# Two-block transformer kernel: the weight split, the exponentials and the scaling of each attention unit cut into halves

## The reference

```python
# first block: 16 query heads, 2 key heads, blocks of 128 queries, window 128, one sink per head
scores = einsum(q, k_window) * 0.125 ; masked to 0 <= i - j < 128
probs  = softmax(concat([scores, sink]))[..., :-1]
out    = einsum(probs, v_window)
# second block: 8 heads, chunks of 64 queries, 576 keys at most, a learned relative bias
scores = einsum(q, k_band) * 0.125 + bias
probs  = softmax(scores) ; out = einsum(probs, v_band)
```

## Time and profile before

| What | Value |
| --- | --- |
| Time of the kernel before, median of 3 runs | 815.47 us (815.34 to 817.68) |
| The profiled execution | 815.34 us, its span 813.6 us |
| TensorE busy | 796.6 us, 98% of the span |
| VectorE busy | 592.4 us, 73% |
| ScalarE busy | 498.6 us, 61% |
| Mean granted TensorE clock | 0.998 of full speed |
| First attention, units 0 to 5 | about 42 to 138 us of the span |
| Second attention, units 6 to 8 | about 571 to 603 us |

### The profile page before, as it was taken

The page is one execution under the profiler, slowest core; times in us unless marked ns, Lnnn a source line. Parts: engine busy times, 40 slices in busy tenths (PEclk is TensorE's granted clock), DMA queues, the critical chain, the costliest instruction groups (busy, mean ns, idle before and its releaser), DMA issues. The chain is left out here.

```text
span 813.6 us, 14276 instructions
## 1 busy us (share of the span) xinstructions
PE 796.6 (98%) x5952; PEld 744.8 (92%) x5952; DVE 592.4 (73%) x772; ACT 498.6 (61%) x752; POOL 15.8 (2%) x36
## 2 busy tenths in 40 slices
PE   8999999999999999999999999999999999999996
PEld 8988879999999889999998889999788999999885
DVE  5575686648766877887878897897768877787463
ACT  6777788568837475344344266856657776666452
POOL 3000000000200000000000000000000000000000
PEclk9999999999999999999999999999999999999999
DMA  8873634446453577889798993635352865646611
GB/s 301 285 252 111 207 104 156 155 155 226 162 183 105 160 254 232 264 292 298 253 300 279 354 358 110 234 133 155 104 173 68 256 205 168 197 137 200 233 52 52
DMA packets 105680, 161.15 MB, mean 198 GB/s; under 512 B 4480, under 2 KB 51856, under 8 KB 105616
## 3 DMA queue, kind: packets, MB, share of 16 engines
q1 hardware_dynamic: 105472, 159.97, 59.8%
q10 hardware_dynamic: 144, 0.26, 0.1%
HBM read 159.16 MB, written 1.06 MB: 197 GB/s over the span
## 5 line engine op out<-in xcount | busy, mean ns | idle before, releaser
L1073 DVE TENSOR_TENSOR wL<-raw,wH 128x2048 fp32r<-128x2048 f32 (+2 forms) x134 | 283.0, 2118 | 122.7 <-ACT wH L695 119.2
L1672 PE MATMUL ps<-p1H,wH 128*128 128x256 f32 x1256 | 359.2, 286 | 1.7 <-DVE p1L L1073 0.8
L1672 PE MATMUL ps<-p1L,wH 128*128 128x256 f32 x1256 | 355.3, 283 | 0.0
L1672 PE MATMUL ps<-p1H,wL 128*128 128x256 f32 x1256 | 355.3, 283 | 0.0
L695 ACT ACTIVATE wH<-raw 128x2048 fp32r<-128x2048 f32 (+1 forms) x120 | 223.1, 1866 | 122.1 <-PE ps L1672 65.9
L1672 PEld LDWEIGHTS ps<-p1H,wH 128*128 128x128 f32 x1256 | 240.8, 192 | 4.8 <-issue 3.5
L1672 PEld LDWEIGHTS ps<-p1L,wH 128*128 128x128 f32 x1256 | 240.9, 192 | 0.3 <-issue 0.2
L1672 PEld LDWEIGHTS ps<-p1H,wL 128*128 128x128 f32 x1256 | 240.8, 192 | 0.0
L1675 PE MATMUL ps<-wH,zH 128*128 128x512 f32 x168 | 65.4, 389 | 0.0
L1675 PE MATMUL ps<-wH,zL 128*128 128x512 f32 x168 | 65.4, 389 | 0.0
L1675 PE MATMUL ps<-wL,zH 128*128 128x512 f32 x168 | 65.4, 389 | 0.0
(11 more groups left out here) (284 smaller groups left out, 974.5 us busy)
## 6 DMA issues: line engine op xcount, KB each, us to landing
raw<-in_w_in SPq DMA_DIRECT2D x37, 1024.0 KB, 5.1
raw<-in_w_ada SPq DMA_DIRECT2D x24, 1024.0 KB, 5.2
raw<-in_w_up SPq DMA_DIRECT2D x44, 512.0 KB, 4.8
raw<-in_w_ffn_gate SPq DMA_DIRECT2D x22, 512.0 KB, 4.5
raw<-in_w_ffn_up SPq DMA_DIRECT2D x22, 512.0 KB, 5.6
raw<-in_w_ffn_down SPq DMA_DIRECT2D x10, 1024.0 KB, 5.3
raw<-in_w_down SPq DMA_DIRECT2D x10, 1024.0 KB, 5.0
raw<-in_w_out SPq DMA_DIRECT2D x8, 1024.0 KB, 5.1
```

The lines of the kernel that those rows point to most:

```text
L1073: return v.tensor_tensor(o, a, b, op)
L1672: last = mm(ps[:, t[1], 0:T], wt[:, slot, k, t[2]:t[2] + P], at_[:, k0 + k, :], start=st, stop=en)
```

## The change

Five edits, all around the attention units; no product, transfer or buffer is added or taken away.

1. In units 0 to 5 the split's ScalarE copy is cut into two of 128 x 1024 (`half_hi`). The first stands where the whole one stood, the second stands behind the exponentials, under a new event ("rest", name, part, u) at the end of `X`. In units 6 to 8 ScalarE still copies the whole panel ahead of the exponentials.
2. In all units but unit 6 the difference on VectorE is cut likewise (`half_lo`): the first half between the maxima and the scaling, the second behind the scaling. `w_lo` is counted up by the second half alone. In unit 6 the difference stays whole.
3. `probs` is raised twice for each unit, after each half of its exponentials, and the sink's exponential (all heads at once) stands between the halves. All waits on `probs` are renumbered.
4. The scaling is done twice, each time for half the heads: `SU + ES` (first attention), reciprocal, and a multiplication of 128 x 512, each raising `pn`.
5. TensorE waits for `pn` before turn 0 and again before turn 4, where it waited once before turn 0; its wait for the yT and pt semaphores now stands ahead.

The diff, cut to its core:

```diff
-HALVED = {("q0", 0): 7, ("out1", 1): 8}
+HALVED = {("q0", 0): 7, ("out1", 1): 14}
...
-                + [("split", name, part), ("scale", u)])
+                + [("split", name, part, u), ("scale", u), ("rest", name, part, u)])
...
+            def half_hi(q, x):
+
+                i = SIDX["w", q]
+                if x == 0:
+                    act.wait_ge(on.raw[i % NRAW], landed[i])
+                    act.wait_ge(*USED[q - NHL])
+                nc.scalar.activation(wH[:, q % NHL, 2 * x:2 * x + 2, :], raw[:, i % NRAW, 2 * x:2 * x + 2, :],
+                                     ACT.Copy).then_inc(on.w_hi if x else on.first_hi, 1)
+
...
                 elif k == "split":
-                    split_hi(PIDX[e[1:]] + AHEAD)
+                    if e[3] < NU1:
+                        half_hi(PIDX[e[1:3]] + AHEAD, 0)
+                    else:
+                        split_hi(PIDX[e[1:3]] + AHEAD)
+                elif k == "rest":
+                    if e[3] < NU1:
+                        half_hi(PIDX[e[1:3]] + AHEAD, 1)
...
-                    ins.then_inc(on.probs, 1)
-                    if kind == 1:
-                        act.wait_ge(on.dsink, u + 1)
-                        nc.scalar.activation(ES[:, u % 2, 0:nh], DS[:, u % 2, 0:nh], ACT.Exp).then_inc(on.esink, 1)
+                        if h % (nh // 2) == nh // 2 - 1:
+                            ins.then_inc(on.probs, 1)
+                        if h == nh // 2 - 1 and kind == 1:
+                            act.wait_ge(on.dsink, u + 1)
+                            nc.scalar.activation(ES[:, u % 2, 0:nh], DS[:, u % 2, 0:nh], ACT.Exp).then_inc(on.esink, 1)
...
+            def half_lo(q, x, u):
+
+                i = SIDX["w", q]
+                if x == 0 and u < NU1:
+                    dve.wait_ge(on.first_hi, KP + 3 + u + 1)
+                else:
+                    dve.wait_ge(on.w_hi, q - AHEAD + 1)
+                ins = tt(wL[:, q % NHL, 2 * x:2 * x + 2, :], raw[:, i % NRAW, 2 * x:2 * x + 2, :],
+                         wH[:, q % NHL, 2 * x:2 * x + 2, :].bitcast(F32), ALU.subtract)
+                if x:
+                    ins.then_inc(on.w_lo, 1)
+
...
                 elif k == "split":
-                    split_lo(PIDX[e[1:]] + AHEAD)
+                    if e[3] == NU1:
+                        split_lo(PIDX[e[1:3]] + AHEAD)
+                    else:
+                        half_lo(PIDX[e[1:3]] + AHEAD, 0, e[3])
+                elif k == "rest":
+                    if e[3] != NU1:
+                        half_lo(PIDX[e[1:3]] + AHEAD, 1, e[3])
...
-                    dve.wait_ge(on.probs, u + 1)
-                    if kind == 1:
-                        dve.wait_ge(on.esink, u + 1)
-                        step(tt(SU[:, u % 2, 0:nh], SU[:, u % 2, 0:nh], ES[:, u % 2, 0:nh], ALU.add))
-                    step(v.reciprocal(RD[:, u % 2, 0:nh], SU[:, u % 2, 0:nh]))
-                    p = PR[u].rearrange("p (h b) n -> p h (b n)", h=nh)
-                    tt(p, p, RD[:, u % 2, 0:nh].unsqueeze(2).broadcast_to([P, nh, nk * P]), ALU.mult).then_inc(on.pn, 1)
+                    for x in range(2):
+                        hs = slice(x * nh // 2, (x + 1) * nh // 2)
+                        dve.wait_ge(on.probs, 2 * u + x + 1)
+                        if kind == 1:
+                            dve.wait_ge(on.esink, u + 1)
+                            step(tt(SU[:, u % 2, hs], SU[:, u % 2, hs], ES[:, u % 2, hs], ALU.add))
+                        step(v.reciprocal(RD[:, u % 2, hs], SU[:, u % 2, hs]))
+                        p = PR[u].rearrange("p (h b) n -> p h (b n)", h=nh)[:, hs]
+                        tt(p, p, RD[:, u % 2, hs].unsqueeze(2).broadcast_to([P, nh // 2, nk * P]),
+                           ALU.mult).then_inc(on.pn, 1)
...
-                        pe.wait_ge(on.probs, u)
+                        pe.wait_ge(on.probs, 2 * u)
...
-                    pe.wait_ge(on.pn, u + 1)
...
                     for b in range(8):
+                        if b % 4 == 0:
+                            pe.wait_ge(on.pn, 2 * u + b // 4 + 1)
                         last = tr(pt67[:, b * P:(b + 1) * P], PR[u][:, b, :])
```

More of the change, by code:

```diff
@@ L1406, in _ @@
                     if u > 1:
-                        dve.wait_ge(on.probs, u - 1)
+                        dve.wait_ge(on.probs, 2 * u - 2)
                     s = sc45[:, 0:nh * nk * P]
@@ L1839, in _ @@
                         pe.wait_ge(on.yT_done, NU1)
-                        pe.wait_ge(on.probs, NU1)
+                        pe.wait_ge(on.probs, 2 * NU1)
                     else:
```

## The result

| | Time, median (range) | Ratio to before, 95% interval |
| --- | --- | --- |
| Before, beside it | 815.9 us (815.28 to 817.68, 6 runs) | |
| After | 810.55 us (809.3 to 812.18, 6 runs) | 0.993 [0.9914, 0.9945] |
| The profiled execution of after | 809.31 us, span 807.6 us, clock 0.997 | |

What follows compares the result with a forecast made beforehand. TensorE, busy 98% of the span, was taken to bound the kernel, so only its waits could be won: 815.34 us minus 5.4 for seven losses, plus 0 and 0, gives 809.9, said as 810.0 us; range 809.0 to 813.3.

Steps and rivals of the forecast that it cites:

- The ceiling: TensorE's turns waiting for VectorE's scaling, six units of the first attention and unit 6: at most 5.4 us to win.
- A loss of up to 0.54 + 0.42 = 0.96 us is gone by this alone: Scaling in halves: last pn 0.54 us earlier, needed only at the fifth turn, 0.42 later; only unit 1 (1.26) lies above.
- The fifth turn's 0.42 us: TensorE needs the last scaled half only for its fifth turn, four turns or 0.42 us after the first.
- The split in halves, 0.5 us in unit 1: ScalarE's halved weight copy ends before the negative maximum, so unit 1's exponentials start 0.5 us earlier.
- The second halves are hidden, 1.3 us to spare in unit 7: Second halves put behind cost nothing; tightest is unit 7, w_lo at 585.8, TensorE at its panel at 587.1.
- Rival 2: Second halves not hidden, panels of units 7 and 8 late: 812.4 us; chance 0.17 together with rival 1 in part.
- The added instructions are free: VectorE's added 0.75 us and ScalarE's 0.2 us a unit stay off the path while chains start with TensorE's scores.
- Rival 1: Added instructions fall on the path, 4.5 us back: 814.6 us; whole or another hiding mechanism 0.14, partly or rival 2 0.17.
- The price of a cut: VectorE's weight difference cut in two: 0.157 us more by the skill's rule, 0.15 by the rows.
- The second wait at 0: TensorE's second wait on pn inside the turns costs 0; upper bound 0.17 us, nine times, 1.5 us.
- Rival 3, late loads: SyncE's loads start later because w_lo comes 2 to 3 us later in six units: 825 us; it or another slower, 0.05.
- The sum: Whole kernel: 815.34 us minus 5.4, plus 0 and 0, gives 809.9; 810.0 us said.

Runs made afterwards that it cites:

- experiment 1: Changed kernel with the weight split whole and ahead again on ScalarE and VectorE, exponentials, scaling and turns still in halves: 814.03 us, ratio 0.9967.
- experiment 3: Changed kernel, but TensorE waits once, ahead of turn 0, for both halves of the scaling: 811.28 us, ratio 0.9945.
- experiment 2: Changed kernel with exponentials, scaling and turns whole again, the weight split still in halves: 814.79 us, ratio 0.9986.
- experiment 6: Changed kernel with the first half of VectorE's weight difference computed two more times in unit 7 alone: 812.33 us, ratio 0.9946.
- experiment 5: Changed kernel with the first half of VectorE's weight difference computed two more times in each of units 0 to 5: 812.82 us, ratio 0.9935.
- experiment 7: Changed kernel, but TensorE waits for pn ahead of each of the eight turns: 811.2 us, ratio 0.9931.
- experiment 8: Changed kernel, second attention's scores wait for each head pair's own k2 tile, not the last ("by pairs"): 810.57 us, ratio 0.9916; run again, 809.03 us.

## Why the prediction was right, and which step of it failed

- *The ceiling*, seven waits for the scaling, 5.4 us: right. All of it was won and nothing came back.
- *"A loss of up to 0.54 + 0.42 = 0.96 us is gone by this alone"*, said of the scaling in halves: wrong. Alone it left 3.45 us (experiment 1). The step took the last multiplication as 0.54 us shorter with the same 0.44 us before it. That holds where ScalarE's last exponential ends last (unit 0, where 0.12 was left of 0.76). Where VectorE itself is late, from its whole difference, the first half's 1.0 us stands in the way and the last half ends 0.4 us later than before. The prediction had seen that units 2, 3 and 5 waited for VectorE's difference, and passed over it because their losses "lie under 0.96 anyway"; of unit 4 it said that it had the pattern of unit 1, and by the rows shown above it had that of units 2, 3 and 5. The second edit covered the error: the halved split takes 1.07 us off VectorE there.
- *The fifth turn's 0.42 us*: it was in the sum for every unit; it is needed in three and worth 0.7 us (experiment 3).
- *The split in halves, 0.5 us in unit 1*: right for the place (the exponentials start 0.04 us after the negative maximum) and nearly for the size (0.41 in experiment 2). Its larger work was in units 2 to 5, where it wins 2.3 of 2.6 us by itself (experiment 2) and the scaling in halves none (experiment 1).
- *The second halves are hidden, 1.3 us to spare in unit 7*: right, 1.44 by the trace, 1.4 by experiment 6. Rival 2 is out.
- *The added instructions are free*: right. VectorE's 3.9 us more did not show, nor did 14.6 more in experiment 5, but for 0.34 in unit 5. Rival 1 is out.
- *The price of a cut*: the rows of the changed kernel, count, busy us and mean ns by form, give 2 x 1222 - 2293 = 151 ns for a difference cut in two. By the rule of the Trainium skill (*VectorE: DVE Perf Modes*, "The TRN2 errata") it is 157, and the trace agrees within 6 ns.

```profile
L1089 DVE TENSOR_TENSOR wL<-raw,wH 128x2048 fp32r<-128x2048 f32 x106 | 242.6, 2293 | 103.6 <-ACT wH L695 103.1
L1089 DVE TENSOR_TENSOR wL<-raw,wH 128x1024 fp32r<-128x1024 f32 x32 | 38.9, 1222 | 11.9 <-ACT wH L695 8.8 <-ACT wH L691 2.7
```

- *The second wait at 0*: right (experiment 7). Its upper bound, 0.17 us each, was the price of a wait that isn't fulfilled.
- *Rival 3, late loads*: no wait for a load of a weight shows in TensorE's waits after the change.
- *The sum*: 810.0 forecast, 810.55 and 810.41 measured. At 0.997 and above the kernel takes 809.3 to 809.4, lower than forecast by the shorter blocks of turns (0.3) and the input's 0.28; at 0.994 and 0.995 it takes 810.2 to 812.2. The forecast took one profiled execution's clock for all, and it is luck that two errors of opposite sign left it within 0.6 us. It is luck too that the wrong step above did no harm: the sum only needed both edits together to clear all seven units.

## What to carry to other kernels

Halving the last step of a chain helps only where the engine that does it has been waiting; where that engine is itself late, the first half's fixed part is added in front, and work of its own must move behind to pay for it. So find for each unit what ends the wait of the last step before summing over units with one number, and when two edits go together, work each out alone. Where the runs of one kernel spread by some microseconds, look at the granted clock stretch by stretch before comparing medians; its mean also counts stretches in which TensorE has nothing to do.

## What the runs showed of the hardware that was not expected

- The TensorE clock fell to 0.50 for up to some 7 us at the same place of the program in some executions and not in others, during or after two blocks of sixteen 32-column products in which TensorE is shown as busy (3.85 us of 4 in the execution of experiment 8, 486 to 490 us). From the turns of unit 0 to those of unit 6 the executions with it took longer by 1.07 us (experiment 6) and, the 0.7 us by pairs allowed for, by 2.6 (experiment 8). Of whole runs before the change the fastest take 814.9 to 815.4 us at 0.998 and 0.999, the slowest 818.4 to 819.8 at 0.993 to 0.995. With 128 columns in these products no run of six was under 0.997. Idle time at that place does not bring it on by itself: in experiment 7 TensorE was busy only 1.28 us of the 2 from 488 to 490 us, and the clock stayed at 1.00 behind it. Why it falls in one execution and not in the next stays open.
- A product of 32, 64 or 128 columns in f32 costs nearly the same at that place: 1.71, 1.74 (485.63 to 487.37 at 64) and 1.79 us for sixteen. Widening to 128 costs 0.08 us a block.
- Eight turns of 128 columns between products of 256 take 0.79 to 0.80 us when they start on time and 0.82 to 0.85 when they start late, so there a wait costs some 0.05 us more than its late start. Behind the scores of the second attention it does not: 0.85 us in unit 7 without a wait, 0.82 to 0.85 in unit 6 with one.
- A fulfilled semaphore wait on TensorE costs nothing that a block of eight shows: 0.79 to 0.80 us with one wait, two, or eight (experiments 3 and 7).
